# SwiGLU feed-forwards of a hybrid encoder: the second step's glue in SBUF, TensorE's fourth step behind its sum, the scaling ahead of VectorE's split of the fourth step's weights

## What is computed

```python
def rms_norm(x, g, eps=NORM_EPS):
    y = xf * lax.rsqrt(jnp.mean(xf * xf, axis=-1, keepdims=True) + eps)
    return y * g

def swiglu(x, w_gate, w_up, w_down):
    return (jax.nn.silu(x @ w_gate) * (x @ w_up)) @ w_down

for layer in range(2):
    x = x + 0.5 * swiglu(rms_norm(x, ffn1_norm[layer]), ffn1_wg[layer], ffn1_wu[layer], ffn1_wd[layer])
    h = rms_norm(x, mix_norm[layer])
    x = x + (hyena_attention_mixer(h, ...) if layer == 0 else rwkv7_bidir_mixer(h, ...))
    x = x + 0.5 * swiglu(rms_norm(x, ffn2_norm[layer]), ffn2_wg[layer], ffn2_wu[layer], ffn2_wd[layer])
```

## Time and profile before

| | us |
|---|---|
| median of 3 runs | 1247.82 (1247.22 to 1248.85) |
| the profiled execution, its own time | 1250.58 |
| its span, from the first to the last instruction | 1248.8 |
| TensorE busy (share of the span) | 1204.4 (96%) |
| VectorE busy | 804.6 (64%) |
| ScalarE busy | 657.7 (53%) |
| GpSimd busy | 404.7 (32%) |
| mean granted TensorE clock | 0.986 of full |

### The profile page before, as it was taken

How to read it: one execution, slowest core, us unless ns; L and a number is a source line. 1 busy time by engine, 2 the same in 40 slices (tenths; PEclk the granted TensorE clock), 3 DMA queues, 4 the chain that set the end, 5 groups by cost and what they waited for, 6 DMA issues and landing times.

```text
span 1248.8 us, 27159 instructions
## 1 busy us (share of the span) xinstructions
PE 1204.4 (96%) x11086; PEld 1086.2 (87%) x11086; DVE 804.6 (64%) x1280; ACT 657.7 (53%) x1118; POOL 404.7 (32%) x218
## 2 busy tenths in 40 slices
PE   8999999988999999999999989997999999999998
PEld 5899999876989999989999979986999888899998
DVE  7655555787685555485555479758777757755554
ACT  5545444664275445474454446665666544654552
POOL 0343443321123443323434410015343412334433
PEclk9999999998999999999999989988999999999999
DMA  9355445422255445554554534411000015554552
GB/s 359 110 194 202 171 182 202 152 102 102 101 205 200 167 185 202 195 199 175 189 201 166 194 146 152 152 51 53 4 4 4 3 59 198 203 193 166 195 190 96
DMA packets 18657, 187.99 MB, mean 151 GB/s; under 512 B 2065, under 2 KB 2577, under 8 KB 3601
## 3 DMA queue, kind: packets, MB, share of 16 engines
q1 hardware_dynamic: 18576, 186.84, 41.2%
HBM read 185.78 MB, written 1.05 MB: 150 GB/s over the span
## 4 chain that ended last, share of the span: by engine, by line
PE 81%; DVE 10%; ACT 6%; issue 1%; POOL 0%; DMA 0%; SPq 0%; DVEq 0%
PE gu_bank L265 24%; PE gu_bank L267 12%; PE bank L244 7%; PE bank L246 7%; PE bank L245 7%; PE bank L1446 7%; PE gu_bank L244 3%; PE gu_bank L1446 3%; PE gu_bank L246 3%; PE gu_bank L245 3%; DVE WL L199 2%; ACT WH L187 2%; PE gu_bank L1477 2%; DVE HX L395 1%; ACT WH L193 1%
## 5 line engine op out<-in xcount | busy, mean ns | idle before, releaser
L208 POOL TENSOR_TENSOR WL<-raw,WH 128x1024 fp32r<-128x1024 f32 x96 | 328.0, 3416 | 595.5 <-ACT WH L193 573.7
L265 PE MATMUL gu_bank<-HX,WH 128*128 128x512 f32 x1408 | 504.0, 400 | 6.4 <-DVE PL L531 4.5
L267 PE MATMUL gu_bank<-HX,WL 128*128 128x256 f32 x1408 | 396.0, 281 | 0.0
L199 DVE TENSOR_TENSOR WL<-raw,WH 128x2048 fp32r<-128x2048 f32 (+1 forms) x114 | 245.1, 2150 | 130.3 <-ACT WH L187 130.3
L265 PEld LDWEIGHTS gu_bank<-HX,WH 128*128 128x128 f32 x1408 | 265.4, 188 | 70.3 <-DVE PL L531 5.1
L267 PEld LDWEIGHTS gu_bank<-HX,WL 128*128 128x128 f32 x1408 | 266.8, 190 | 0.2
L187 ACT ACTIVATE WH<-raw 128x2048 fp32r<-128x2048 f32 (+1 forms) x114 | 205.0, 1799 | 26.5 <-PE gu_bank L246 14.4
L244 PE MATMUL bank<-PH,WH 128*128 128x256 f32 (+1 forms) x720 | 201.7, 284 | 1.0 <-ACT arena L2043 0.9
L245 PE MATMUL bank<-PL,WH 128*128 128x256 f32 (+1 forms) x720 | 201.6, 283 | 0.0
L246 PE MATMUL bank<-PH,WL 128*128 128x256 f32 (+1 forms) x720 | 201.5, 283 | 0.0
L452 ACT ACTIVATE work<-gu_bank 128x512 f32<-128x512 f32 x88 | 52.5, 597 | 168.3 <-PE gu_bank L267 168.3
(11 more groups left out here) (313 smaller groups left out, 1811.5 us busy)
## 6 DMA issues: line engine op xcount, KB each, us to landing
raw<-stream_in SPq DMA_DIRECT2D x114, 1536.0 KB, 6.5
cst<-const_in SPq DMA_DIRECT2D x1, 1568.0 KB, 17.8
X<-xT_in SPq DMA_DIRECT2D x1, 1024.0 KB, 6.1
raw<-stream_in SPq DMA_DIRECT2D x1, 1024.0 KB, 8.1
arena<-hconst_in SPq DMA_DIRECT2D x2, 512.0 KB, 11.4
out<-X SPq DMA_DIRECT2D x4, 256.0 KB, 2.1
arena<-hconst_in SPq DMA_DIRECT2D x1, 768.0 KB, 14.5
arena<-fw_in SPq DMA_DIRECT2D x1, 512.0 KB, 8.9
```

Of the source, the lines that this page charges most:

```text
L199: nc.vector.tensor_tensor(WL[:, slot, :cut], raw[:, slot, :cut], WH[:, slot, :cut].bitcast(fp32), ALU.subtract).then_inc(lo_ready, 1)
L208: (eng or nc.gpsimd).tensor_tensor(WL[:, slot, cut:end], raw[:, slot, cut:end], WH[:, slot, cut:end].bitcast(fp32), ALU.subtract).then_inc ...
L265: nc.tensor.matmul(out[:, :], WH[:, slot, w:w + P], HX[:, x, :, :].rearrange("p i t -> p (i t)"), start=k == 0, stop=False)
L267: return nc.tensor.matmul(out[:, L:2 * L], WL[:, slot, w:w + P], HH[:, x, :], start=False, stop=k == CT - 1)
```

## The change

Three things are changed, all in the opening of a feed-forward.

1. `glue_tiles`: the second step's sum, too, lies in SBUF (`gus[1]`), and its product in `prod[:, 1, :]`. That is so in all four feed-forwards.
2. `step`: the fourth step's first matmul waits for the second step's sum (`gsum_ready`) in place of its `PL`, and the wait on `pl_ready` stands ahead of the down block, as it did in the third step. The fourth and fifth step are written out, and the loop runs over the other sixteen.
3. `dve_ffn`: `rest` is cut in two, `scaled` (the scaling, L526 before) and `gated_low` (product and `PL`). For `n` > 0 the second step's scaling stands ahead of the split of piece `s0 + 3`, the fourth step's weights; its product and `PL` stay behind it.

```diff
             def step(f, o, first=False):
                 s, slot = s0 + f, (p0 + o) % 2
                 pe.wait_ge(lo_ready, s + 1)
-                if first:
-                    pe.wait_ge(gsum_ready, q0 + 1)
+                if isinstance(f, int) and f < 4:
+                    pe.wait_ge(gsum_ready, q0 + f - 1)
                 else:
                     pe.wait_ge(pl_ready, q0 + f - 1)
...
                 pe.wait_ge(lo_last, s + 1)
-                if first:
-                    pe.wait_ge(pl_ready, q0 + 1)
+                if isinstance(f, int) and f < 4:
+                    pe.wait_ge(pl_ready, q0 + f - 1)
...
             step(2, 0, first=True)
-            with pe.Fori(0, (FT - 4) // 2) as i:
+            step(3, 1)
+            step(4, 0)
+            with pe.Fori(0, (FT - 6) // 2) as i:
                 for u in range(2):
-                    step(2 * i + (3 + u), (1 + u) % 2)
+                    step(2 * i + (5 + u), (1 + u) % 2)
             step(FT - 1, (FT - 1) % 2)
...
         def glue_tiles(f, o):
 
-            if isinstance(f, int) and f == 0:
-                return gus[0], prod[:, 0, :]
+            if isinstance(f, int) and f < 2:
+                return gus[f], prod[:, f, :]
             return gu_bank[:, o, :, 0:L], gu_bank[:, o, 0, 0:L]
...
-            def rest(f, o):
+            def scaled(f, o):
                 if isinstance(f, int) and f == 0:
                     dve.wait_ge(rstd_ready, n + 1)
-                gated, product = glue_tiles(f, o)
+                gated, _ = glue_tiles(f, o)
                 dve.wait_ge(gsum_ready, q0 + f + 1)
                 nc.vector.tensor_tensor(gated, gated, both, ALU.mult).then_inc(gs_ready, 1)
+
+            def gated_low(f, o):
+                gated, product = glue_tiles(f, o)
                 dve.wait_ge(sg_ready, q0 + f + 1)
                 dve.wait_ge(gs_ready, q0 + f + 1)
                 nc.vector.tensor_tensor(product, sg[:, o, :], gated[:, 1, :], ALU.mult).then_inc(prod_ready, 1)
                 dve.wait_ge(ph_ready, q0 + f + 1)
                 nc.vector.tensor_tensor(PL[:, o, :], product, PH[:, o, :].bitcast(fp32), ALU.subtract)\
                     .then_inc(pl_ready, 1)
+
+            def rest(f, o):
+                scaled(f, o)
+                gated_low(f, o)
...
             else:
                 sums(1, 1)
+                scaled(1, 1)
                 next_lo(dve, s0 + 3)
-                rest(1, 1)
+                gated_low(1, 1)
                 sums(2, 0)
                 next_lo(dve, s0 + 4)
                 rest(2, 0)
```

## The result

The changed kernel takes **1251.71 us** (median of 19 runs, 1249.04 to 1256.74), against 1247.82 us (median of 19 runs, 1243.27 to 1252.83) for the kernel before, taken in turns with it: a ratio of 1.003, 95% interval 1.0018 to 1.0042. It is slower by 3.9 us. The profiled execution took 1252.27 us, 1250.5 of it span, at a mean granted clock of 0.989 (before: 1250.58 us, 1248.8, 0.986).

What follows compares the result with a forecast made beforehand. The prediction took TensorE, busy 1204.4 of 1248.8 us, as the bound. On the median of 1247.8 us it added 1.5 for longer stalls and 2.2 for clock falls, giving 1251.5 us, range 1247.9 to 1254.0.

Steps and rivals of the forecast that it cites:

- Who goes first: Fourth step's weights: GpSimd asks inside the moved scaling, goes at its end; VectorE's split, 2.28 us before, takes about 4.4.
- rival 4: Scaling doesn't hold GpSimd off; wait on PL becomes one on the weights, +0.1 us each, 1248.1 us; chance 0.05.
- The size of the stall: Ahead of the fourth step in the second to fourth feed-forward: +0.5 us each, +1.5 in all, stalls 1.95 to 2.1.
- What comes late: Third step's PL comes 1.8 us later, with 0.9 us to spare: no new stall ahead of the fifth step.
- The clock: TensorE's granted clock falls behind one or two of the three stalls, 1.5 us each: +2.2 us, bounds 0 to 4.5.
- The sum: Whole kernel: stalls 1.5 plus clock 2.2, +3.7 us on the median of 1247.8, giving 1251.5 us.
- Rival 1: No port conflict: VectorE's split follows its scaling directly, the three stalls vanish, -4.5 us, 1243.3 us; chance 0.12.
- Rival 2: Port conflict at the three stalls, but the clock holds: +1.5 us, 1249.3 us; chance 0.28.
- Rival 3: Port conflict, and clock falls after all three stalls or third step's PL is late too: 1253.8 us; chance 0.15.

Runs made afterwards that it cites:

- f_ask_behind_scaling: Changed kernel with GpSimd's part of the fourth step's weights waiting, in the second to fourth feed-forward, for the second step's scaling: 1247.36 us, ratio 0.9994.
- b_pool_after: Changed kernel with GpSimd's part of the fourth step's weights waiting, in the second to fourth feed-forward, for VectorE's split: 1242.37 us, ratio 0.9952.
- c_move_only: Kernel before with only the scaling moved ahead of the split; second step's glue stays in PSUM, TensorE's fourth step waits for PL: 1255.72 us, ratio 1.0068.
- d_sbuf_only: Kernel before with only the second step's glue put in SBUF; scaling stays behind the split, fourth step waits for PL: 1260.35 us, ratio 1.0101.
- g_fill: Changed kernel with four useless matmuls in TensorE's stall ahead of the fourth step of the second to fourth feed-forward: 1250.10 us, ratio 1.0026.
- h_gate_on_product: Changed kernel with the scaling back behind VectorE's split and GpSimd's part of the fourth step's weights waiting for the second step's product: 1244.61 us, ratio 0.9980.
- a_no_move: Changed kernel with the scaling put back behind VectorE's split; glue in SBUF and TensorE's wait on the sum stay: 1250.83 us, ratio 1.0021.
- e_gate_no_move: Changed kernel with the scaling back behind VectorE's split and GpSimd's part of the fourth step's weights waiting for that split: 1246.45 us, ratio 0.9985.

## Why the prediction was right, point by point

**Who goes first.** Right, and shown. The forecast turned on one step: GpSimd asks inside the moved scaling, goes at its end, and the split is held. The rows of the kernel after have it (4.49 us predicted near 4.4, GpSimd 2.69 predicted near 2.65), f_ask_behind_scaling shows that the moment of asking is the cause, b_pool_after that nothing else was in the way. The request came 0.99 us after the sum's start (361.10 - 360.11), as predicted. The glue in SBUF, which the prediction names as part of the reason, isn't needed for it: c_move_only has the glue in PSUM and the split is held all the same, as the prediction's rival 4 had it.

**The size of the stall.** Predicted +0.5 us at each place; the fourth step starts 0.57 us later in each of the three (23.13, 23.12 and 23.14 against 22.56), +1.7 in all against the predicted +1.5. The held split ended at GpSimd's end plus 2.15, which is its own 2.28 less 0.13, near the 0.15 taken from the L419 and L1824 pairs. The stalls that the trace prints grew more, by 0.71, because TensorE was there 0.14 us sooner. Those 0.14 us are no effect of the change that the runs show. c_move_only and the kernel after stand ready 20.81 and 20.82 us behind the first L265, the kernel before and d_sbuf_only both 20.96, but the difference is there by the end of the second step, and there it doesn't follow the move: with the move, f_ask_behind_scaling and g_fill are as late as the kernel before, and h_gate_on_product, without it, is as early as the kernel after (the L267 that starts 11.23 us behind the first L265 before and 11.08 after starts at 11.26, 11.24 and 11.08 in these). What makes them isn't found. They end in the wait, so they gain nothing.

**What comes late.** Right: no wait ahead of the fifth step. `PL` is done at 373.70, 0.81 us ahead of that step's start (0.9 predicted). How near it was, a_no_move, e_gate_no_move and f_ask_behind_scaling show, where the same `PL` is the wait.

**The clock.** Predicted: falls behind one or two of the three stalls, 1.5 us each, +2.2 in all. The price is shown; how many falls the median execution has isn't; and what the prediction took that number from, the length of the stall, turned out not to tell.

The price first. From the fourth feed-forward's first L265 to the end the kernel before takes 193.78 us, the kernel after, with its fall, 195.92. The same stretch of g_fill and of c_move_only:

```profile
1053.80:1248.10 194.30, 190.29 (x1242) 173.00 (x1242) 112.55 (x130) 95.38 (x121) 69.24 (x20) 1.00 0.48 176
...
1056.87:1253.60 196.73, 190.12 (x1234) 172.92 (x1234) 112.23 (x130) 95.46 (x121) 68.89 (x20) 0.99 0.48 174
```

g_fill's fourth step is as late as that of the kernel after (23.14 us behind the first L265 in both, before 22.56) and has no fall: the fall costs 195.92 - 194.30 = 1.6 us. In c_move_only the stretch is 2.95 us longer than before, 1.51 of it delay (24.07 - 22.56), which leaves 1.4 for the fall; in d_sbuf_only 3.50 and 2.21, which leaves 1.3.

Then the length. The profiled execution has its one fall behind a stall of 2.14 us, while stalls of 2.31 and 2.15 us had none. And the stall of the first mixer that the prediction took as an example, 1.85 us at 282.96, stands in ten of the eleven profiles, 1.85 or 1.86 us long: behind it the clock fell in five (before, a_no_move, d_sbuf_only, e_gate_no_move, g_fill) and stayed at 1.00 in the other five, the kernel after among them:

```profile
282.81 0.33 PE L905 MATMUL bank<-cst,arena 128*128 128x128 f32 x1 [1.86 <-DVE arena L1155]
```

Its other example, the stall of 1.75 us at 756.70, is 1.75 to 2.19 us long in five profiles, all with a fall, and 2.64 to 2.99 in the other six, all without. So between 1.8 and 3 us the length alone doesn't say whether the clock falls, and 1.60 against 1.75 us was no border. That one and a half falls came near is in part luck.

How many falls the median has can only be argued from means over all timed runs. Over 20 runs of the kernel before (those beside a_no_move and b_pool_after) the granted clock is 0.9904 in the mean, over the 19 of the kernel after 0.9883. At two levels, 1.00 and 0.50, a mean of 0.9904 over 1249 us is 2 x 0.0096 x 1249 = 24 us at half clock, and 0.9883 over 1250 us is 29 us, 5 us more. At 1.5 us per 3.3 us, the price of the prediction, they cost 2.3 us, and 1.7 + 2.3 = 4.0 us against 3.9 measured. But the kernel before has 0.9913 in the 27 runs beside g_fill and 0.9917 in the 23 beside h_gate_on_product. With the mean of all 70, 0.9912, the same sum gives 7 us more at half clock, 3.3 us, and 5.0 in all. The sign is clear, the size isn't; and h_gate_on_product, with no stall over 0.4 us at the fourth and fifth step, has a mean of 0.9892, so a low mean need not come from these three stalls. That falls stand behind them is shown for one of them in one execution.

In c_move_only and d_sbuf_only, with stalls of 3.0 to 4.0 us, the clock fell at all three. A window of c_move_only behind its third stall (behind the first and second 0.51 too):

```profile
1082.60:1085.60 3.00, 3.00 (x11) 2.60 (x10) 2.85 (x2) 1.06 (x2) 1.86 (x1) 0.51 0.87 369
```

The same sum made for these two: c 3 x 1.49 + 3 x 1.5 = 9.0 us, measured 7.6; d 3 x 2.22 + 3 x 1.5 = 11.2, measured 12.2 (the fourth step's delay taken from the second feed-forward for all three). With a fall at each of the three stalls the sum is off by 1.4 and 1.0 us.

**The sum.** The forecast was 1.5 + 2.2 on 1247.8, 1251.5 us, and 1251.71 was measured. The 1.5 is shown, as 1.7. The 2.2 that is left (3.9 less 1.7) is a difference and no measurement of the clock: g_fill, with the same delay and no fall in its profile, still lies 2.6 us above the kernel before, 0.9 more than the delay. So the agreement of the second term is good in direction and partly luck in size.

**The rivals.** Rival 1 (no conflict, 1243.3) is what b_pool_after makes by hand, 1242.37. Rival 2 (conflict, clock holds, 1249.3) is wrong for the profiled execution, which has the fall; g_fill, which comes nearest to it, took 1250.10, and for the median execution the clock means speak against it without settling it. Rival 3 (three falls) is c_move_only and d_sbuf_only, not the change. Rival 4 wanted GpSimd let in at once, which c_move_only shows (2.40 us); with both inputs in SBUF it isn't.

**What stays open.** The share of the three stalls behind which the clock falls over many executions, and what decides it; the cause of the 0.14 us; and how much of the 2.2 us beyond the delay is clock.

## What to carry to other kernels

Before moving a VectorE operation with two SBUF inputs, look for GpSimd's next request beside it and ask which of the two is then first: the loser waits for what is left of the other's length (2.2 us here), so a move of 0.7 us can cost 2.2 us at the instruction that matters. Give the loss to the operation with the most slack by making GpSimd wait for a chosen point, and judge slack by everything queued behind the victim on other engines too: here the product carried ScalarE's next weights, and `PL` carried nothing urgent. A stall that disappears from the list of waits is not gone until the list has been read again for a new name in the same place.

## What the runs showed of the hardware that was not expected

- Half a microsecond in the time of a request decides 2.2 us. With VectorE's split issued at 361.95 and GpSimd's L208 at 362.11 the split takes 2.28 us; with GpSimd at 361.10 and the split at 361.45, 4.49.
- A VectorE operation with one PSUM input didn't keep GpSimd out (2.40 us for L208), one with two SBUF inputs did (2.69), and the split that was issued 0.35 us later was held in either case (4.20 and 4.49).
- The length of a stall didn't say whether the clock falls behind it: one stall of 1.85 us in the first mixer lost it in five profiles and kept it in five, another kept it in all six profiles in which it was 2.64 to 2.99 us long and lost it in all five in which it was 1.75 to 2.19. The six between 3.0 and 4.0 us at the fourth step of c_move_only and d_sbuf_only all lost it.
- One fall to the 1.2 GHz level cost 1.3 to 1.6 us in the fourth feed-forward (195.92 against 194.30 us with the same delay and the stall filled).
- Over 19 executions of one kernel the time spread by 7.7 us with nothing changed.
